# State products with the chunk-masked operand on the moving side of the matmul

## The reference, cut to what matters

```python
def step(S, inp):                       # per row t, for each of 16 heads of 64
    r_t, d_t, k_t, v_t, kk_t, a_t = inp
    Skk = einsum('bhvk,bhk->bhv', S, kk_t)
    S = S * d_t[:, :, None, :] - Skk[..., None] * (kk_t * a_t)[:, :, None, :] + v_t[..., None] * k_t[:, :, None, :]
    return S, einsum('bhvk,bhk->bhv', S, r_t)
S_final, y = lax.scan(step, wkv_prev, seq)
```

## Time and profile before

| | |
|---|---|
| median of 3 executions | 3208.07 us (3204.24 to 3215.23) |
| the profiled execution: its own time | 3212.12 us |
| its span in the trace | 3210.3 us |
| mean granted TensorE clock | 0.823 of 2.4 GHz |
| PE, DVE, ACT, POOL busy | 67%, 56%, 21%, 33% |
| read from HBM | 992.71 MB |

### The profile page before, as it was taken

The page is one execution under the profiler, slowest core; times in us unless marked ns, Lnnn a source line. Parts: engine busy times, 40 slices in busy tenths (PEclk is TensorE's granted clock), DMA queues, the critical chain, the costliest instruction groups (busy, mean ns, idle before and its releaser), DMA issues. The chain is left out here.

```text
span 3210.3 us, 33248 instructions
## 1 busy us (share of the span) xinstructions
PE 2136.8 (67%) x11625; PEld 1143.0 (36%) x11625; DVE 1785.2 (56%) x4126; ACT 678.3 (21%) x1920; POOL 1054.6 (33%) x990
## 2 busy tenths in 40 slices
PE   6949658482477686748567585676767758655555
PEld 3418557270144253423224232233224434322222
DVE  1043343337786675675665765746744454965555
ACT  1012121010221321211421112411213221121111
POOL 0004122003356463333333333333233223354442
PEclk9979789696688798879778797788868878878787
DMA  5230100345889999999999999899999999999998
GB/s 168 97 137 1 68 13 6 119 133 217 342 309 390 375 393 403 420 400 393 402 371 420 395 398 402 351 412 417 371 414 392 420 404 409 360 385 421 420 420 336
DMA packets 152820, 1019.55 MB, mean 318 GB/s; under 512 B 17872, under 2 KB 18944, under 8 KB 37456
## 3 DMA queue, kind: packets, MB, share of 16 engines
q0 software_dynamic: 117024, 825.84, 64.0%
q1 hardware_dynamic: 35632, 191.58, 15.2%
HBM read 992.71 MB, written 18.39 MB: 315 GB/s over the span
## 5 line engine op out<-in xcount | busy, mean ns | idle before, releaser
L1328 PE MATMUL fl_acc<-fl_pairs,fl_diag 128*64 128x512 f32 x2576 | 826.5, 744 | 459.9 <-ACT fl_diag L1301 427.7
L1355 POOL DMA_INDIRECT fl_pairs<-in_peer_uv,fl_row_at x644 | 726.5, 1128 | 1132.6 <-PE fl_acc L1328 1015.4
L1281 DVE CUSTOM_DVE_ANT_0 fl_pairs<-fl_pairs,fl_rows 128x1024 f32<-128x1024 f32 x644 | 785.5, 1239 | 410.7 <-DMA fl_pairs<-in_peer_uv,fl_row_at 409.5
L1328 PEld LDWEIGHTS fl_acc<-fl_pairs,fl_diag 128*64 128x64 f32 x2576 | 283.7, 162 | 879.3 <-issue 815.4
L1307 ACT ACTIVATE fl_acts<-fl_dots 128x2 f32<-128x2 f32 x384 | 78.5, 205 | 1260.0 <-DVE fl_dots L1281 1259.3
L1301 ACT ACTIVATE fl_diag<-constants_sb,fl_mix 128x64 f32<-128x64 f32 x768 | 225.1, 343 | 319.2 <-DVE fl_mix L1271 314.3
L1328 PE MATMUL fl_acc<-fl_more,fl_diag 128*64 128x512 f32 x496 | 171.2, 786 | 138.5 <-ACT fl_diag L1301 121.8
L1355 POOL DMA_INDIRECT fl_more<-in_peer_uv,fl_row_at x124 | 144.0, 1161 | 263.3 <-PE fl_acc L1328 241.9
L1281 DVE CUSTOM_DVE_ANT_0 fl_more<-fl_more,fl_rows 128x1024 f32<-128x1024 f32 x124 | 150.0, 1225 | 115.2 <-DMA fl_more<-in_peer_uv,fl_row_at 114.9
L1786 PE MATMUL aacc<-pc_ring,at_xT 128*128 128x512 f32 x288 | 141.7, 637 | 15.9 <-PEq L1713 15.9
L1328 PEld LDWEIGHTS fl_acc<-fl_more,fl_diag 128*64 128x64 f32 x496 | 61.0, 168 | 218.8 <-issue 209.6
(11 more groups left out here) (509 smaller groups left out, 2898.0 us busy)
## 6 DMA issues: line engine op xcount, KB each, us to landing
pc_ring<-in_kvq_by_pair SPq DMA_DIRECT2D x36, 1024.0 KB, 9.2
pc_ring<-in_query_by_head SPq DMA_DIRECT2D x32, 1024.0 KB, 9.8
pc_ring<-in_past_k SPq DMA_DIRECT2D x16, 1024.0 KB, 14.3
pc_ring<-in_past_v SPq DMA_DIRECT2D x16, 1024.0 KB, 13.6
w_ring<-in_rwkv_w_rkv SPq DMA_DIRECT2D x24, 512.0 KB, 3.3
pc_ring<-in_out_by_pair SPq DMA_DIRECT2D x12, 1024.0 KB, 9.6
fl_pairs<-in_peer_uv,fl_row_at POOLq DMA_INDIRECT x644, 15.8
fl_pairs<-in_query_by_head SPq DMA_DIRECT2D x8, 1024.0 KB, 10.3
```

The lines of the kernel that those rows point to most:

```text
L1281: dve.tensor_tensor_reduce(pair, pair, self.rows[:, u % 2, j, :], 1.0, 0.0, ALU.mult, ALU.add, self.dots[:, u % 2, q, j:j + 1]).then_inc(* ...
L1328: mm = pe.matmul(self.acc[j * FOLD:(j + 1) * FOLD, half, :], self.diag[:, self.summed % self.DIAGS, j, :], self.pair(g)[:, D + half * HALF ...
L1355: pool.indirect_dma_start(self.pair(g), None, self.io["peer_uv"], bass.IndirectOffsetOnAxis(ap=self.row_at[:, u % TILES, j, q:q + 1], axis ...
```

## The change

The masks move from the weights to the moving operand. With E = B_end or K_end unmasked as weights, one matmul of 512 columns gives all eight chunks of a head: column block c of the moving operand is x (or v) with all rows but chunk c's set to zero. POOL masks v where it masked K_end, with the same instructions. `B_by_chunk` stays, since the state factors read it. The masked x is new: in the prompt tiles DVE makes it in eight instructions a group, in the sample's halves ACT does.

```diff
-        B_by_chunk, K_by_chunk = sb("B_by_chunk", [P, GH, NCH, N]), sb("K_by_chunk", [P, GH, NCH, N])
+        B_by_chunk, v_by_chunk, x_by_chunk = (sb(n, [P, GH, NCH, N]) for n in ("B_by_chunk", "v_by_chunk", "x_by_chunk"))
...
                 def state_terms(g, q):
                     pe.wait_ge(*(q1_done, y2_done)[q].at(g + 1))
-                    for c in range(NCH):
+                    pe.wait_ge(*x_spread.at(g + 1))
+                    for end, by_chunk_of in ((w["B_end"], x_by_chunk), (w["K_end"], v_by_chunk)):
                         for h in (2 * q, 2 * q + 1):
-                            out = bank[6 + q][half(h), c * N:(c + 1) * N]
-                            pe.matmul(out, B_by_chunk[:, h, c, :], x[:, g % 2, 0, h, N:], start=True, stop=False, tile_position=(0, h % 2 * N))
-                            mm = pe.matmul(out, K_by_chunk[:, h, c, :], v[:, head(g, h)], start=False, stop=True, tile_position=(0, h % 2 * N))
+                            mm = pe.matmul(bank[6 + q][half(h), :], end[:, head(g, h)], by_chunk_of[:, h].rearrange("p c n -> p (c n)"),
+                                           start=(by_chunk_of is x_by_chunk), stop=(by_chunk_of is v_by_chunk), tile_position=(0, h % 2 * N))
                     mm.then_inc(*gp.by())
...
                     if back:
                         add(b, 3)
+                        dve.wait_ge(*x_done.at(4 * b + 4))
+                        if b > 0:
+                            dve.wait_ge(*gp.at(GP * b))
+                        for c in range(NCH):
+                            ins = dve.tensor_scalar(x_by_chunk[:, :, c, :], x[:, b % 2, 0, :, N:], core.const("chunk")[:, c:c + 1], None, ALU.mult)
+                        ins.then_inc(*x_spread.by())
                         dve.wait_ge(*q1.at(b + 1))
...
-                        for dst, src in ((B_by_chunk, w["B_end"]), (K_by_chunk, w["K_end"])):
+                        for dst, src in ((B_by_chunk, w["B_end"]), (v_by_chunk, v)):
```

In `half_chunks` the tiles, the state terms (one bank, two heads) and POOL's operand change in the same way, and ACT gets the masks:

```diff
                     if back:
                         act.wait_ge(*y2.at(b + 1))
                         act.copy(x.Y2t[:, b, :], bank[5][:, 0:P]).then_inc(*y2_done.by())
+                        if b > 0:
+                            act.wait_ge(*gp.at(b))
+                        for c in range(NCH):
+                            ins = act.activation(x_by_chunk[:, :, c, :], y[:, b % 2, 0, :, N:], ACT.Copy, scale=core.const("chunk")[:, c:c + 1])
+                        ins.then_inc(*x_spread.by())
                     if front:
                         power(g, 2, m4t[:, g % 2], 0, 2 * P)
```

More of the change, by code:

```diff
@@ L502, in wkv_chunks @@
         fp, fp_done, gp, gp_done = core.sig("fp"), core.sig("fp_done"), core.sig("gp"), core.sig("gp_done")
-        a_copied, zeroed = core.sig("a_copied"), core.sig("zeroed")
+        a_copied, zeroed, x_spread = core.sig("a_copied"), core.sig("zeroed"), core.sig("x_spread")
         quad = lambda b, n: b[:, 0:GH * n].rearrange("p (h n) -> p h n", h=GH)
@@ L2621, in state_terms @@
                     pe.wait_ge(*y2_done.at(g + 1))
-                    for c in range(NCH):
+                    pe.wait_ge(*x_spread.at(g + 1))
+                    for end, by_chunk_of in ((x.B_end, x_by_chunk), (x.K_end, v_by_chunk)):
                         for h in range(GH):
-                            out = bank[5][half(h), c * N:(c + 1) * N]
-                            pe.matmul(out, B_by_chunk[:, h, c, :], y[:, g % 2, 0, h, N:], start=True, stop=False, tile_position=(0, h * N))
-                            mm = pe.matmul(out, K_by_chunk[:, h, c, :], x.v[:, head(g, h)], start=False, stop=True, tile_position=(0, h * N))
+                            mm = pe.matmul(bank[5][half(h), :], end[:, head(g, h)], by_chunk_of[:, h].rearrange("p c n -> p (c n)"),
+                                           start=(by_chunk_of is x_by_chunk), stop=(by_chunk_of is v_by_chunk), tile_position=(0, h * N))
                     mm.then_inc(*gp.by())
@@ L2808, in _ @@
                         for h in range(GH):
-                            for dst, src in ((B_by_chunk, x.B_end), (K_by_chunk, x.K_end)):
+                            for dst, src in ((B_by_chunk, x.B_end), (v_by_chunk, x.v)):
                                 pool.tensor_tensor(dst[:, h], src[:, head(b, h)].unsqueeze(1).broadcast_to([P, NCH, N]), spread, ALU.mult).then_inc(*exp_done.by())
-                                flow.gpsimd(pool, tick + 1 + 2 * h + (dst is K_by_chunk))
+                                flow.gpsimd(pool, tick + 1 + 2 * h + (dst is v_by_chunk))
                     else:
```

## The result

The changed kernel takes 3216.09 us, median of 20 runs, beside 3207.87 us for the kernel before in 20 runs on the same chip: ratio 1.0026 with the interval 1.0017 to 1.0036, some 8.2 us slower. The prediction said 3207.4 us, 3200 to 3215. The median lies 1 us above the range. The forecast was a gain of 0.7 us and the kernel lost 8.2, which is 0.26%, under the 0.3% that the prediction counted as none.

What follows compares the result with a forecast made beforehand. Gathers bound the kernel from 1200 us on; before that, stages run in sequence and PE's path in the prompt counts. Terms -3.0 + 0.3 + 2.0 = -0.7 us on 3208.1 gave 3207.4 us, range 3200 to 3215.

Steps and rivals of the forecast that it cites:

- Part 1: PE's state-term calls in the prompt tiles: 2.06 to 1.87 us each, 16 calls, -3.0 us; bounds 0 to some 5.
- Part 2: DVE's eight masks a group in the prompt tiles: 2.9 us, hidden except in last iterations, +0.3 us for two tiles.
- The upper bound of 2.0 us a tile: Prompt tiles: DVE's masks waiting for both POOL instructions, at most 2.0 us more a tile, 4 in all; nothing taken.
- Part 3: POOL masks v in place of K_end with the same instructions and shape: no change in time.
- Part 4: ACT's eight masks a group in the sample: 2.5 us a group, mostly hidden, +2.0 us, bounds 0 and 26.
- DVE's queue at the first group of half 0: Sample, group of 922 us: DVE is busy 5.00 of 5.00 us, so its queue is the limit and covers ACT's delay.
- The first, all groups uncovered: Rival: ACT's masks uncovered in most sample groups, 20 us less 3, 3225 us; decides if DMA share under 1; chance 0.06.
- below 0.95 would prove the forecast wrong: Sign in the sample's second half: DMA share between 1110 and 1200 us, 0.99 before, falling below 0.95 refutes the prediction.
- The second rival: Prompt tiles: DVE's masks, held up by POOL, delay Q1t in last iterations; 4 us given back, 3209 to 3212; chance 0.13.

Runs made afterwards that it cites:

- the prompt part alone: Prompt tiles as changed, sample's halves as in the kernel before: 3200.63 beside 3206.45 us, ratio 0.9982 to the kernel before.
- mid: Changed kernel with ACT's eight sample masks moved behind the copy of m4t, ahead of the diagonals: 3214.91 us, ratio 1.0030 to the kernel before.
- the dose: Changed prompt tiles, sample of before plus unread ACT masks: four a group 3207.45 us, ratio 1.0001; eight a group 3215.02 us, 1.0026.
- early: Changed kernel with ACT's sample masks moved ahead of its wait for DVE's dots: 3200.74 us, 0.9986 to the kernel before; repeat 3200.55 us, 0.9985.
- late: Changed kernel with ACT's sample masks moved behind the diagonals of the same tick and the next copy: 3207.32 us, ratio 1.0003 to the kernel before.
- the sample's part in its early place: Kernel before's prompt tiles, changed sample with ACT's masks ahead of its wait for dots: 3200.50 us, 0.9983; repeat 3203.02 us, 0.9992.

## Why the prediction was wrong

- **Part 1 held**, mechanism and size: 8 records of 128x512, 1.87 us to the next block, as forecast from L601. Columns are what is paid here. By the spacings of the Trainium skill, "TensorE: Matmul & The Clock Gate", section "Back-to-back issue gap", the call would have taken about half, by an estimate from its 131 ns at 512 columns (8 x 131 ns = 1.05 us). The trace has 234 ns for each fp32 record, and the rule was set aside on the right row. The stage gained 4.1 us by the profiles' means, 1.4 us more than the 2.7 of parts 1 and 2. The executions say 5.8 us for the prompt part alone, with an interval of 2 to 10 us that holds both.
- **Part 2 held in the middle and was sized too small at the ends.** The eight masks took 2.19 us, under the 2.9 taken, and hid. In the last iterations they took 3.40 and 3.92 us: 1.2 and 1.7 us more, beside POOL's two instructions, for which I had taken nothing. The Trainium skill, "SBUF — State Buffer", section "Who interferes with whom", says that of a tensor_scalar in a two-port mode and a GpSimd instruction the one that comes first blocks the other for a whole instruction. The trace agrees on DVE's side, where single masks take up to 1298 ns beside a median of 346; POOL's longest of these instructions is 1093 ns beside 1042, and in which mode the masks ran no run shows. I had put +0.3 us, and PE's waits there come to 0 and 0.99 us, the 0 at half the clock. The upper bound of 2.0 us a tile was not reached.
- **Part 3 held**: POOL's busy time is 1055.0 us after 1054.6.
- **Part 4 is the step that failed.** The masks' own size was right, 2.44 us a group for 2.5. The cover was wrong. "In the second half it is 0.99 over 1110 to 1200 us, the transfers are queued up, and a delay of 2.5 us in issuing some of them is hidden": I put +2.0 us, and the masks cost 14. My own upper bound for them was 26 us, and the range up to 3215 left it out. The limit there was not the transfers but PE's own queue, whose next instruction waits for m4t or the diagonals: PE's waits for m4t went from 3.8 to 15.7 us. The DMA share could cover nothing, since the gathers of the halves are bound to the ticks: 128 MB in every run, so that the longer stage lowers the share (0.99, 0.95 and 0.90 in this window). In half 1, said to be covered, the group grew from 21.5 to 23.7 us, by 2.1 of the 2.44. One cover of the prediction held, DVE's queue at the first group of half 0: the next one came 33.5 us later, after 33.3. That the diagonals or what is queued with them suffice is shown by mid, that the loss grows with the masks' number by the dose, and that it isn't ACT's time but its place by early. That the end moves by what PE waited is my reading of the table and of the stages.
- **The rivals.** The first, all groups uncovered, was right in kind and too high in price: 20 us less 3, where 14 less 6 came. I gave it 0.06, with the DMA share as the condition from which it decides. It was the wrong condition, as the halves' mean share only went from 0.94 to 0.91 and followed the length of the stage. The share had been named as the test as well (below 0.95 would prove the forecast wrong), and it came out at 0.95: a test too blunt, since 14 us in 350 need a mean share only 0.04 lower. The second rival, a wait in the prompt in place of the gain, came in part, with 0.99 us in one tile, and the gain stood. The better question was in the earlier trace rows already: what does ACT hand over behind this point, and does somebody wait for it?

**What stays open.** Why well-placed masks in the sample gained 0.0017 and 0.0008 with the old prompt tiles, and nothing on top of the new ones: all these intervals overlap, and the difference isn't in the halves (347 and 354 us in the two profiles, 347 before), so that neither a gain nor a cause is settled. Why the prompt part's 5.8 us seem to be more than the stage's 4.1. And why late's halves are as long as mid's in its one profile, when its time is 8 us better. Of the versions run, early (0.9986 and 0.9985), the prompt part alone (0.9982) and the sample's part in its early place (0.9983 and 0.9992) are the best, by too little to choose between them.

## What to carry to other kernels

Before work is added to an engine's queue, list what stands behind that point and who waits for it. Here one block of 2.4 us, run eight times, cost 14 us in one place and nothing a few lines further up, where the engine waited anyway. A DMA share near 1 isn't a cover when the program binds the transfers to its own ticks: here the stage moved the same 128 MB however long it took, and the share fell because the stage grew. Ask first whether the engines wait for the data at all. And in fp32, these few wide matmuls in place of many narrow ones with the same columns gained only 9% of the call.

## What the hardware showed unexpectedly

POOL's tensor_tensor held up DVE's tensor_scalar even with each in its own tiles: eight masks of 128 x 256 took 2.19 us alone, 3.40 and 3.92 beside two of POOL's, which kept their 1.05 us each. It was the same in the sample, where DVE would be the quicker engine for the masks of 128 x 128: 1.66 us for eight with no mask of POOL beside them, where ACT takes 2.44, but up to 4.06 in other groups.
